# Gated blocks of a feed-forward net turned by VectorE squares and small DMAs in place of TensorE transposes

## The chip, the cores and the metric

One Trainium2 chip, one of its cores. The metric is the device time of one execution in microseconds. The kernel before takes 972.12 us, the median of three runs (972.08 to 974.28). The profile shown is of one further execution, which took 969.86 us.

## The reference, cut to what matters

The kernel computes a two-layer decoder trunk for 256 tokens of width 1024 in float32: a state-space layer and an attention layer, each between two half-weighted SwiGLU feed-forward nets (inner width 2816). The change touches only the four feed-forward nets:

```
def swiglu(x, w_in, w_out):
    g, u = jnp.split(x @ w_in, 2, axis=-1)
    return (jax.nn.silu(g) * u) @ w_out
...
h = h + 0.5 * swiglu(rmsnorm(h, ffn1_norm[layer]), ffn1_w_in[layer], ffn1_w_out[layer])
```

## The kernel before, in words

The work is a list of 13 phases, each a product of the 256 tokens with one streamed weight matrix. Four phases are called "in" (n = 0, 3, 7, 11: x @ w_in, 11 blocks of 512 columns, 8 tiles of the inner dimension) and each is followed by an "out" phase (n = 1, 4, 8, 12: @ w_out, 2 blocks, 22 tiles). Weights come in units of 128 x 1024 floats (two tiles of one block). An "in" block has 4 units, an "out" block 11.

Each float32 product is made of three products of fp32r parts. For each unit SyncE loads 512 KB into one of six `raw` buffers (L412), ScalarE writes the high part `w_hi` (`split`, L652), VectorE the rest `w_lo` (`split`, L931), and TensorE runs 12 matmuls for it (2 token halves x 2 tiles x 3 products, L1252). There are four slots for `w_hi` and `w_lo`. In each unit's step, ScalarE and VectorE split the unit that is three further on (`LEAD = 3`), and ScalarE waits first until TensorE has used the unit that had the slot before.

The order on each engine is written out by hand, as a loop over phase, block and unit. In the step of unit 0 of a block, ScalarE takes silu of the gate half of the block before from PSUM, once for each half of the tokens (`gate`, L672), and VectorE multiplies it with the other half and the inverse RMS into `prod` (`gated`, L970). `prod` has tokens on the partitions. The "out" phase needs it with the inner columns on the partitions, as `hid_hi` and `hid_lo`. Before the change TensorE does this: after unit 1 of blocks 4 and 8, and after unit 1 of the "out" phase, it transposes the last four (at the end three) blocks in a batch (`turn_hidden`, L1257: eight 64 x 128 transposes a block). ScalarE copies the PSUM result to `hid_hi` in fp32r (`high_hidden`, L680) and VectorE writes the difference to `hid_lo` (`low_hidden`, L982), spread over the steps after.

ScalarE's queue is in order: what is issued in one step stands ahead of all later splits. The state-space part lies between phases 1 and 2, and its tables are made by GpSimd, ScalarE and VectorE during phases 0 and 1.

Of the kernel before, what the change touches and what calls it, by code (L numbers as in the profile page):

```python
# [11 lines left out]
ALU = mybir.AluOpType  # L12
ACT = mybir.ActivationFunctionType
# [3 lines left out]

P = 128
HP = P // 2
TOK = 256  # L20
TT = TOK // P
D = 1024
# [42 lines left out]

X_OF = {2: [(2, 1)], 4: [(3, 0), (4, 1)], 8: [(5, 0)], 10: [(6, 0)]}
FINAL = 12
BATCH = 4
BATCHES = (0, 4, 8)
TABLE_AT = (1, 3, 5, 7, 9, 11, 12, 13, 14, 15, 16, 17)  # L70


# [35 lines left out]
    return [(phases[p.n - 1], phases[p.n - 1].blocks - 1, j)] if chained else []  # L108


def batch_behind(p, phases, b):

    if p.name == "in" and b in BATCHES[1:]:
        return p, range(b - BATCH, b)
    if p.name == "out" and b == 0:
        f = phases[p.n - 1]
        return f, range(BATCHES[-1], f.blocks)
    return p, range(0)


def high_behind(p, phases, b, j):

    if p.name == "in" and b in BATCHES[1:] and j >= 2:
        first = b - BATCH + 2 * (j - 2)
        return [(p, first), (p, first + 1)]
    if p.name == "out" and b == 0 and j in (2, 3):
        f = phases[p.n - 1]
        first = BATCHES[-1] + 2 * (j - 2)
        return [(f, c) for c in range(first, min(first + 2, f.blocks))]
    return []  # L130


def low_behind(p, phases, b, j):

    if p.name == "in" and b in BATCHES[1:] and j == 3:
        return [(p, b - BATCH)]
    if p.name == "in" and b - 1 in BATCHES[1:] and j >= 1:
        return [(p, b - 1 - BATCH + j)]
    if p.name == "out" and b == 0 and 3 <= j < 3 + phases[p.n - 1].blocks - BATCHES[-1]:
        return [(phases[p.n - 1], BATCHES[-1] + j - 3)]  # L140
    return []


def trunk(nc, io, out):
# [9 lines left out]
    def sem(name):  # L154
        return ctx.enter_context(nc.semaphore(name))

    with ctx:
# [99 lines left out]
        def w_columns(d):  # L257
            return w2[:, :, :, PPT * d:PPT * d + PPT, :].rearrange("p r s g j -> p (r s) g j")

        def prod_of(b):  # L260
            i = b % BATCH
            return prod[:, i] if i < 2 else prod2[:, i - 2]

        def halves(a):
            return a.rearrange("p (b h x) -> p b h x", h=2, x=HP)

        def turned_block(b):
            at, col = KT + b % BATCH // 2 * 2, b % 2 * HB
            return ps[:, at:at + 2, col:col + HB].rearrange("p h (b x) -> p b h x", x=HP)

        def z_place(d):
            i = d % Z_SLOTS
# [17 lines left out]
        def bank(gb, tok):  # L290
            return 2 * ((gb + 1) % 2) + tok
# [9 lines left out]
        drained = sem("drained")  # L301
        kq_drained = sem("kq_drained")
        act_ready = sem("act_ready")
        hid_turned = sem("hid_turned")
        hid_hi_done = sem("hid_hi_done")
        hid_ready = sem("hid_ready")

# [330 lines left out]
        def _(act):  # L638
# [7 lines left out]
            def split(gu):  # L646
                if gu >= len(units):
                    return
                act.wait_ge(landed[gu % RAW], 16 * (gu // RAW + (1 if gu % RAW else 0)))
                if gu >= WS:  # L650
                    act.wait_ge(unit_used, gu - WS + 1)
                act.activation(w_hi[:, gu % WS, :], raw[:, gu % RAW, :], ACT.Copy)\  # L652
                   .then_inc(hi_done, 1)
# [8 lines left out]
            def gate(p, b):  # L662
                for q in range(TT):
# [10 lines left out]
                    else:  # L674
                        act.activation(act_out[:, q, :], ps[:, bank(p.block0 + b, q), HB:NB],
                                       ACT.Sigmoid).then_inc(act_ready, 1)

            def high_hidden(p, b):
                act.wait_ge(hid_turned, p.hid0 + min(b // BATCH * BATCH + BATCH, p.blocks))
                act.activation(halves(hid_hi[:, 2 * b:2 * b + 2, :].rearrange("p f x -> p (f x)")),  # L680
                               turned_block(b), ACT.Copy).then_inc(hid_hi_done, 1)

            def squares(p, b, w):
                for q in range(TT):
# [44 lines left out]
            def dense(n, chained=True):  # L729
                p = phases[n]  # L730
                for b in range(p.blocks):
                    for j in range(p.upb):
                        for done in follow_ups(p, phases, b, j, chained):
                            after(*done)
                        for turned_one in high_behind(p, phases, b, j):
                            high_hidden(*turned_one)
                        if j < p.upb - (LEAD if n == 1 and b else 0) and (n, b, j) not in SPLIT_IN_S5:
                            split(p.unit0 + b * p.upb + j + LEAD)
                        if n == 0 and b == 0 and j == 3:
                            input_squares()  # L740
                        if n == 0 and b == 1 and j == 1:
                            s5_angles()
                        if n == 1 and b == 1 and 3 <= j < 3 + len(early_masks):
                            early_masks[j - 3]()
# [174 lines left out]
        def _(dve):  # L919
# [41 lines left out]
            def gated(p, b):  # L961
                for q in range(TT):
                    dve.wait_ge(act_ready, p.acts0 + TT * b + q + 1)
                    gb = p.block0 + b
                    if p.name == "in":
                        if b >= BATCH:
                            dve.wait_ge(hid_turned, p.hid0 + b - BATCH + 1)
                        elif p.hid0:
                            dve.wait_ge(hid_turned, p.hid0)
                        dve.scalar_tensor_tensor(prod_of(b)[:, q, :], ps[:, bank(gb, q), HB:NB],  # L970
                                                 rs[:, q:q + 1], act_out[:, q, :],
                                                 ALU.mult, ALU.mult).then_inc(drained, 1)
                    else:
                        cols = slice(HB * b, HB * b + HB)
                        link(dve.tensor_tensor(prod[:, 0, q, :], ps[:, bank(gb, q), 0:HB],
                                               act_out[:, q, :], ALU.mult))
                        dve.tensor_tensor(h[:, q, cols], h[:, q, cols], prod[:, 0, q, :], ALU.add)\
                           .then_inc(drained, 1)

            def low_hidden(p, b):  # L980
                dve.wait_ge(hid_hi_done, p.hid0 + min(b // 2 * 2 + 2, p.blocks))
                dve.tensor_tensor(halves(hid_lo[:, 2 * b:2 * b + 2, :].rearrange("p f x -> p (f x)")),  # L982
                                  turned_block(b),
                                  halves(hid_hi[:, 2 * b:2 * b + 2, :].rearrange("p f x -> p (f x)")
                                         .bitcast(F32)), ALU.subtract).then_inc(hid_ready, 1)

            def residual(p, b):
                for q in range(TT):
# [261 lines left out]
        def _(pe):  # L1250
# [3 lines left out]
            def turn(at, col, src):  # L1254
                for r in range(2):
                    rows = slice(HP * r, HP * r + HP)
                    last = pe.transpose(ps[:, at + r, col:col + HP], src[rows, :], ident[rows, rows])  # L1257
                return last

            def turn_hidden(f, batch):  # L1260
                if not batch:
                    return
                pe.wait_ge(drained, f.drained0 + TT * (batch[-1] + 1))
                if f.hid0 + batch[0]:
                    pe.wait_ge(hid_ready, f.hid0 + batch[0])
                if f.n == 7 and batch[0] == 0:
                    pe.wait_ge(kq_ready, 4)
                for b in batch:
                    for i in range(2):
                        for q in range(TT):  # L1270
                            last = turn(KT + b % BATCH // 2 * 2, b % 2 * HB + (2 * i + q) * HP,
                                        prod_of(b)[:, q, i * P:i * P + P])
                    last.then_inc(hid_turned, 1)

            def turn_h(p, c):

                t = turned[p.n, c]
# [70 lines left out]
            def dense(n, chained=True):  # L1348
                p = phases[n]
                for b in range(p.blocks):  # L1350
                    late = p.upb - left(p, b)
                    if (n, b) == (2, 0):
                        continue
                    for j in range(2 if (n, b) == (10, 0) else 0, p.upb):
                        if j == late:
                            for q in range(TT):
                                for i in range(late, p.upb):
                                    unit(p, b, i, (q,))
                        if j >= late:
                            continue  # L1360
                        unit(p, b, j)
                        for done in follow_ups(p, phases, b, j, chained):
                            after(*done)
                        if j == 1:
                            turn_hidden(*batch_behind(p, phases, b))
                        if n == 9 and b == 1 and j >= 2:
                            scores(j - 2)

# [249 lines left out]
```

## Time and profile before

| | |
|---|---|
| Median of three runs | 972.12 us |
| The profiled execution, its own time | 969.86 us |
| Its span in the trace | 967.7 us |
| TensorE busy (matmul) | 955.9 us, 99% |
| VectorE busy | 597.8 us, 62% |
| ScalarE busy | 499.8 us, 52% |
| GpSimd busy | 189.5 us, 20% |
| Queue of SyncE's loads | 167.79 MB, 54.5% of the 16 DMA engines' time |

The span is what the trace covers; 2.2 us of the execution's time lie around it. TensorE is busy almost throughout, so its matmuls are the line against which the others' delays count. An engine's share is a mean over stages: ScalarE and VectorE have idle time in each unit, and an instruction that makes DMAs counts as no busy time of its engine.

### The profile page before, as it was taken

The page shows a single profiled execution, that of the slowest core. Times are in us where ns is not written, and L with a number is a line of the kernel's source. Part 1 is how long each engine was busy: PE and PEld are TensorE (multiplying, and loading weights), DVE is VectorE, ACT ScalarE, POOL GpSimd, SP SyncE. Part 2 cuts the span into 40 slices and gives each one's busy share as a digit, 9 for nine tenths or more (in the row PEclk, how much of TensorE's full clock was granted, in tenths as well). Part 3 has the DMA queues.
Part 4 walks back from the last instruction along what each step waited for, and adds up shares of the span by engine and source line. Part 5 has one row for each costly group of instructions (what it writes and reads, how often), then busy time and mean ns, then how long its engine had stood idle before and what let it go on. Part 6 is the DMA issues. An engine that isn't in the chain of part 4 may idle for free.

```text
span 967.7 us, 15102 instructions
## 1 busy us (share of the span) xinstructions
PE 955.9 (99%) x6110; PEld 790.2 (82%) x6110; DVE 597.8 (62%) x744; ACT 499.8 (52%) x711; POOL 189.5 (20%) x235
## 2 busy tenths in 40 slices
PE   9999999999999999999999999999999999999997
PEld 7888888788788888888888888888888888888886
DVE  5565779889765554656555555555557555656544
ACT  7554544576555454545544454554458454545441
POOL 4899999800000000000000000000060000000000
PEclk9999999999999999999999999999999999999999
DMA  9766555520455655565566666656651366555551
GB/s 347 269 184 197 181 174 174 175 69 5 142 187 193 194 178 194 184 208 183 166 198 196 193 177 196 191 177 195 188 182 45 111 198 193 186 187 192 179 169 43
DMA packets 47557, 169.35 MB, mean 175 GB/s; under 512 B 5505, under 2 KB 5505, under 8 KB 47489
## 3 DMA queue, kind: packets, MB, share of 16 engines
q1 hardware_dynamic: 47056, 167.79, 54.5%
q8 instruction: 48, 0.79, 0.3%
q10 hardware_dynamic: 432, 0.61, 0.2%
q14 instruction: 21, 0.16, 0.1%
HBM read 167.33 MB, written 1.05 MB: 174 GB/s over the span
## 4 chain that ended last, share of the span: by engine, by line
PE 88%; DVE 8%; issue 2%; ACT 1%; DMA 1%; SPq 0%; POOLq 0%; POOL 0%; DVEq 0%; ACTq 0%
PE ps L1252 85%; DVE w_lo L931 2%; PE ps L1257 2%; DVE scan L1158 1%; DVE tmp L1087 1%; PE ps L1284 1%; DMA raw<-in_in 1%; DVE rot_b L1165 1%; DVE rot_a L1145 1%; DVE rot_b L1147 1%; ACT w_hi L652 0%; DVE rot_in L1154 0%; DVE states L1172 0%; PE ps L1297 0%; ACT pr L881 0%
## 5 line engine op out<-in xcount | busy, mean ns | idle before, releaser
L931 DVE TENSOR_TENSOR w_lo<-raw,w_hi 128x1024 fp32r<-128x1024 f32 x311 | 399.7, 1289 | 307.0 <-ACT w_hi L652 305.7
L652 ACT ACTIVATE w_hi<-raw 128x1024 fp32r<-128x1024 f32 x311 | 328.4, 1059 | 305.9 <-PE ps L1252 303.2
L1252 PE MATMUL ps<-w_hi,x_hi 128*128 128x512 f32 x896 | 352.4, 393 | 0.9 <-DVE w_lo L931 0.6
L1252 PE MATMUL ps<-w_hi,x_lo 128*128 128x512 f32 x896 | 349.3, 390 | 0.0
L1252 PE MATMUL ps<-w_lo,x_hi 128*128 128x512 f32 x896 | 349.2, 390 | 0.0
L1252 PEld LDWEIGHTS ps<-w_hi,x_hi 128*128 128x128 f32 x896 | 168.4, 188 | 37.2 <-DVE w_lo L931 1.4
L1252 PEld LDWEIGHTS ps<-w_hi,x_lo 128*128 128x128 f32 x896 | 168.3, 188 | 35.2
L1252 PEld LDWEIGHTS ps<-w_lo,x_hi 128*128 128x128 f32 x896 | 168.5, 188 | 34.0
L1252 PE MATMUL ps<-w_hi,hid_hi 128*128 128x512 f32 x352 | 138.1, 392 | 1.0 <-DVE w_lo L931 1.0
L1252 PE MATMUL ps<-w_lo,hid_hi 128*128 128x512 f32 x352 | 137.2, 390 | 0.0
L1252 PE MATMUL ps<-w_hi,hid_lo 128*128 128x512 f32 x352 | 137.2, 390 | 0.0
L466 POOL TENSOR_TENSOR ms<-ss 128x2 f32<-128x2 f32 x5 | 1.0, 203 | 528.6 <-ACT act_out L689 525.0
L1252 PEld LDWEIGHTS ps<-w_hi,hid_hi 128*128 128x128 f32 x352 | 66.1, 188 | 16.0 <-DVE w_lo L931 2.3
L1252 PEld LDWEIGHTS ps<-w_hi,hid_lo 128*128 128x128 f32 x352 | 66.1, 188 | 13.9
L1252 PEld LDWEIGHTS ps<-w_lo,hid_hi 128*128 128x128 f32 x352 | 66.1, 188 | 13.4
L672 ACT ACTIVATE act_out<-ps,rs 128x256 f32<-128x256 f32 x88 | 41.5, 475 | 45.5 <-PE ps L1252 45.4
L970 DVE SCALAR_TENSOR_TENSOR prod<-ps,rs,act_out 128x256 f32<-128x256 f32 x88 | 41.8, 480 | 19.7 <-ACT act_out L672 19.7
L680 ACT ACTIVATE hid_hi<-ps 128x512 fp32r<-128x512 f32 x44 | 24.1, 599 | 32.0 <-PE ps L1257 32.0
L634 POOL TENSOR_TENSOR rs<-end_ms,mhalf 128x1 f32<-128x1 f32 x2 | 1.1, 560 | 182.3 <-DVE end_ms L1241 182.3
L466 POOL TENSOR_TENSOR sm<-sm 128x32 f32<-128x32 f32 x64 | 34.3, 536 | 11.0 <-ACT sm L793 3.8
L982 DVE TENSOR_TENSOR hid_lo<-ps,hid_hi 128x512 fp32r<-128x512 f32 x44 | 30.0, 682 | 0.0
L466 POOL TENSOR_TENSOR tmp<-cp,sm 128x512 f32<-128x512 f32 x16 | 26.2, 1637 | 1.3
(151 smaller groups left out, 599.6 us busy)
## 6 DMA issues: line engine op xcount, KB each, us to landing
raw<-in_in SPq DMA_DIRECT2D x175, 512.0 KB, 4.3
raw<-in_out SPq DMA_DIRECT2D x88, 512.0 KB, 3.4
raw<-in_glu SPq DMA_DIRECT2D x16, 512.0 KB, 4.3
raw<-in_k SPq DMA_DIRECT2D x8, 512.0 KB, 4.4
raw<-in_v SPq DMA_DIRECT2D x8, 512.0 KB, 4.1
raw<-in_q SPq DMA_DIRECT2D x8, 512.0 KB, 4.4
raw<-in_o SPq DMA_DIRECT2D x8, 512.0 KB, 4.0
xt<-in_xt SPq DMA_DIRECT2D x4, 256.0 KB, 5.6
```

The lines of the kernel that those rows point to most:

```text
L466: link(pool.tensor_tensor(o, a, b, op))
L652: act.activation(w_hi[:, gu % WS, :], raw[:, gu % RAW, :], ACT.Copy)\
L672: act.activation(act_out[:, q, :], ps[:, bank(p.block0 + b, q), 0:HB], ACT.Silu, scale=rs[:, q:q + 1]).then_inc(act_ready, 1)
L680: act.activation(halves(hid_hi[:, 2 * b:2 * b + 2, :].rearrange("p f x -> p (f x)")), turned_block(b), ACT.Copy).then_inc(hid_hi_done, 1)
L931: dve.tensor_tensor(w_lo[:, gu % WS, :], raw[:, gu % RAW, :], w_hi[:, gu % WS, :].bitcast(F32), ALU.subtract)\
L970: dve.scalar_tensor_tensor(prod_of(b)[:, q, :], ps[:, bank(gb, q), HB:NB], rs[:, q:q + 1], act_out[:, q, :], ALU.mult, ALU.mult).then_inc( ...
L982: dve.tensor_tensor(halves(hid_lo[:, 2 * b:2 * b + 2, :].rearrange("p f x -> p (f x)")), turned_block(b), halves(hid_hi[:, 2 * b:2 * b + 2 ...
L1087: link(dve.tensor_tensor(part[k], t[:, groups, low], turn[i], ALU.mult))
L1145: dve.tensor_tensor(rot_a[:, :, :, :], v, table(rotc, d), ALU.mult)\
L1147: dve.tensor_tensor(rot_b[:, :, :, :], v, table(rots, d), ALU.mult)\
L1252: return pe.matmul(o, w, x, start=start, stop=stop, skip_group_check=True)
L1257: last = pe.transpose(ps[:, at + r, col:col + HP], src[rows, :], ident[rows, rows])
```

## The change

TensorE's transposes of the gated blocks (`turn_hidden`) are gone. A gated block of 256 x 256 is now turned in two steps. VectorE transposes the block's 32 x 32 squares in place, with one instruction of 128 x 512 elements at the end of `gated`; for this it first waits for its own two products of the block. Then ScalarE issues sixteen DMAs from SBUF to SBUF (`move_hidden`), one for each pair of 32-partition groups; each has 32 partitions x 4 runs x 32 floats (16 KB in runs of 128 bytes). They put the squares at their places in `hid_lo`. ScalarE issues them one unit after the step in which the block was gated, that is after the split in the step of unit 1 (in the first "in" phase the first block's are two units later). Four semaphores, one for each slot of the four blocks in flight, count the landings.

`high_hidden` now waits for a block's sixteen DMAs and reads `hid_lo` in SBUF; `low_hidden` subtracts in place in `hid_lo`. Both now come for one block at a time, in units 1 and 2 of the block two further on; the last two blocks of a phase in units 1 and 2 and units 4 and 5 of the "out" phase. `gated` waits for the DMAs of the block four before.

```diff
+def gate_unit(p, b):
+    return (b + 1) * p.upb + (2 if p.n == 0 and b == 0 else 0)
+
+def high_behind(p, phases, b, j):
+    if p.name == "in" and b >= 2 and j == 1:
+        return [(p, b - 2)]
+    if p.name == "out" and b == 0 and j in (1, 4):
+        return [(f, f.blocks - 2 + j // 4)]
...
+        def pieces(g, q, c):
+            return prod_of(g)[Q * q:Q * q + Q].rearrange("p t (a c x) -> p c (t a) x", a=2, x=Q)[:, c]
+        def places(b, q, c):
+            return hid_lo[Q * c:Q * c + Q, 2 * b:2 * b + 2, :].bitcast(F32)\
+                .rearrange("p i (t q x) -> p q (i t) x", t=TT, x=Q)[:, q]
...
+            def move_hidden(p, b):
+                g = p.hid0 + b
+                act.wait_ge(hid_squares, g + 1)
+                for q in range(QS):
+                    for c in range(QS):
+                        act.dma_start(places(b, q, c), pieces(g, q, c)).then_inc(hid_moved[g % SLOTS], 16)
+            moves = {p.unit0 + gate_unit(p, b) + MOVE_BEHIND: (p, b)
+                     for p in phases if p.name == "in" for b in range(p.blocks)}
             def high_hidden(p, b):
-                act.wait_ge(hid_turned, p.hid0 + min(b // BATCH * BATCH + BATCH, p.blocks))
-                act.activation(halves(hid_hi[...]), turned_block(b), ACT.Copy).then_inc(hid_hi_done, 1)
+                act.wait_ge(hid_moved[g % SLOTS], 16 * QS * QS * (g // SLOTS + 1))
+                act.activation(hid_hi[:, 2 * b:2 * b + 2, :], hid_lo[:, 2 * b:2 * b + 2, :].bitcast(F32),
+                               ACT.Copy).then_inc(hid_hi_done, 1)
...
                         if j < p.upb - (LEAD if n == 1 and b else 0) and (n, b, j) not in SPLIT_IN_S5:
                             split(p.unit0 + b * p.upb + j + LEAD)
+                        if p.unit0 + b * p.upb + j in moves:
+                            move_hidden(*moves[p.unit0 + b * p.upb + j])
...
+                if p.name == "in":
+                    dve.wait_ge(drained, p.drained0 + TT * (b + 1))
+                    whole = prod_of(p.hid0 + b).rearrange("p t x -> p (t x)")
+                    dve.transpose(whole, whole).then_inc(hid_squares, 1)
...
-                        if j == 1:
-                            turn_hidden(*batch_behind(p, phases, b))
```

## Rows read from the trace of the kernel before

**Rows 1.** The page: busy time, share of the span and instructions of each engine.

```profile
PE 955.9 (99%) x6110; PEld 790.2 (82%) x6110; DVE 597.8 (62%) x744; ACT 499.8 (52%) x711; POOL 189.5 (20%) x235
```

**Rows 2.** The chain in order of time: start us, us, what.

```profile
136.56 0.92 PE ps L1257 x16
...
338.78 1.15 PE ps L1257 x32
339.93 43.74 PE ps L1252 x192
...
417.70 0.90 PE ps L1257 x24
```

**Rows 3.** Most of phase 3: us, busy of PE, PEld, DVE, ACT, POOL, clock, DMA share, GB/s.

```profile
292.50:418.00 125.50, 125.50 (x617) 103.44 (x615) 70.51 (x77) 62.73 (x78) 1.08 (x4) 1.00 0.60 193
```

**Rows 4.** Waits in that stretch: us in total, times, longest us.

```profile
ACT w_hi L652 <- PE ps L1252: 44.1, 29, 1.7
```

**Rows 5.** Timeline of ScalarE: start us, us, line, operation.

```profile
333.38 0.47 ACT L672 ACTIVATE act_out<-ps,rs 128x256 f32<-128x256 f32 x1 [0.88 <-PE ps L1252]
333.75 1.05 ACT L652 ACTIVATE w_hi<-raw 128x1024 fp32r<-128x1024 f32 x1
336.16 1.06 ACT L652 ACTIVATE w_hi<-raw 128x1024 fp32r<-128x1024 f32 x1 [1.35 <-PE ps L1252]
...
340.94 1.06 ACT L652 ACTIVATE w_hi<-raw 128x1024 fp32r<-128x1024 f32 x1
341.89 1.08 ACT L680 ACTIVATE hid_hi<-ps 128x512 fp32r<-128x512 f32 x2
```

**Rows 6.** Timeline of VectorE in the same phase.

```profile
331.81 1.23 DVE L931 TENSOR_TENSOR w_lo<-raw,w_hi 128x1024 fp32r<-128x1024 f32 x1 [1.49 <-ACT w_hi L652]
332.95 0.48 DVE L970 SCALAR_TENSOR_TENSOR prod<-ps,rs,act_out 128x256 f32<-128x256 f32 x1
333.89 0.48 DVE L970 SCALAR_TENSOR_TENSOR prod<-ps,rs,act_out 128x256 f32<-128x256 f32 x1 [0.46 <-ACT act_out L672]
...
342.03 1.23 DVE L931 TENSOR_TENSOR w_lo<-raw,w_hi 128x1024 fp32r<-128x1024 f32 x1 [3.56 <-ACT w_hi L652]
```

**Rows 7.** SyncE's loads (min/median/max ns), then ScalarE's queue of DMAs beside its work.

```profile
L412 SPq DMA_DIRECT2D raw<-in_out x88: 327/328/328, 109.5 to 936.8; - x88
...
409.64 1.06 ACT L652 ACTIVATE w_hi<-raw 128x1024 fp32r<-128x1024 f32 x1 [1.66 <-PE ps L1252]
409.66 0.34 ACTq L871 DMA_DIRECT2D last_gain<-in_last_gain  x1
```

**Rows 8.** Timeline of SyncE's issues at the start, one behind the other.

```profile
2.17 0.43 SPq L416 DMA_DIRECT2D xt<-in_xt  x1
...
3.59 0.54 SPq L412 DMA_DIRECT2D raw<-in_in  x1
...
4.69 1.80 SPq L412 DMA_DIRECT2D raw<-in_in  x3
...
15.33 0.65 SPq L426 DMA_DIRECT2D w<-in_b  x1
16.02 0.60 SPq L426 DMA_DIRECT2D w<-in_c  x1
```

**Rows 9.** DMA queues from 2 to 4 us, then from 340 to 383 us.

```profile
q10 hardware_dynamic: 163, 0.04, 9.5%
...
q1 hardware_dynamic: 2192, 8.00, 57.8%
```

**Rows 10.** Issues of the whole run: KB each, median us to landing.

```profile
raw<-in_in SPq DMA_DIRECT2D x175, 512.0 KB, 4.3
...
out_x<-fin SPq DMA_DIRECT2D x4, 256.0 KB, 2.2
```

**Rows 11.** Groups by shape that stand for the new work.

```profile
L982 DVE TENSOR_TENSOR hid_lo<-ps,hid_hi 128x512 fp32r<-128x512 f32 x44 | 30.0, 682 | 0.0
L1158 DVE TENSOR_TENSOR_SCAN scan<-decay_even,rot_in 128x512 f32<-128x512 f32 x4 | 4.9, 1225 | 0.1
```

More of the change, by code:

```diff
@@ L19 @@
 HP = P // 2
+Q = 32
+QS = P // Q
 TOK = 256
@@ L67 @@
 FINAL = 12
-BATCH = 4
-BATCHES = (0, 4, 8)
+SLOTS = 4
+MOVE_BEHIND = 1
 TABLE_AT = (1, 3, 5, 7, 9, 11, 12, 13, 14, 15, 16, 17)
@@ L108, in follow_ups @@
     return [(phases[p.n - 1], phases[p.n - 1].blocks - 1, j)] if chained else []
[L111 to L115, printed above, removed]
-        f = phases[p.n - 1]
[L117 to L129, printed above, removed]
+def gate_unit(p, b):
[4 more added lines that the diff above has]
+    if p.name == "out" and b == 0 and j in (1, 4):
+        f = phases[p.n - 1]
+        return [(f, f.blocks - 2 + j // 4)]
     return []
 def low_behind(p, phases, b, j):
[L135 to L140, printed above, removed]
+    if p.name == "in" and b >= 2 and j == 2:
+        return [(p, b - 2)]
+    if p.name == "out" and b == 0 and j in (2, 5):
+        f = phases[p.n - 1]
+        return [(f, f.blocks - 2 + j // 5)]
     return []
@@ L258, in w_columns, with prod_of, tile_of @@
             return w2[:, :, :, PPT * d:PPT * d + PPT, :].rearrange("p r s g j -> p (r s) g j")
[L260 to L261 removed]
+        def prod_of(g):
+            i = g % SLOTS
             return prod[:, i] if i < 2 else prod2[:, i - 2]
+        def tile_of(g, q):
+            return prod_of(g).rearrange("p i (t x) -> p t i x", x=P)[:, q]
+        def pieces(g, q, c):
[3 more added lines that the diff above has]
+                .rearrange("p i (t q x) -> p q (i t) x", t=TT, x=Q)[:, q]
         def halves(a):
             return a.rearrange("p (b h x) -> p b h x", h=2, x=HP)
[L267 to L269 removed]
         def z_place(d):
@@ L303, in trunk @@
         act_ready = sem("act_ready")
-        hid_turned = sem("hid_turned")
+        hid_squares = sem("hid_squares")
+        hid_moved = [sem(f"hid_moved{i}") for i in range(SLOTS)]
         hid_hi_done = sem("hid_hi_done")
@@ L676, in gate @@
                                        ACT.Sigmoid).then_inc(act_ready, 1)
+            def move_hidden(p, b):
[6 more added lines that the diff above has]
+                     for p in phases if p.name == "in" for b in range(p.blocks)}
             def high_hidden(p, b):
-                act.wait_ge(hid_turned, p.hid0 + min(b // BATCH * BATCH + BATCH, p.blocks))
-                act.activation(halves(hid_hi[:, 2 * b:2 * b + 2, :].rearrange("p f x -> p (f x)")),
-                               turned_block(b), ACT.Copy).then_inc(hid_hi_done, 1)
+                g = p.hid0 + b
+                act.wait_ge(hid_moved[g % SLOTS], 16 * QS * QS * (g // SLOTS + 1))
+                act.activation(hid_hi[:, 2 * b:2 * b + 2, :], hid_lo[:, 2 * b:2 * b + 2, :].bitcast(F32),
+                               ACT.Copy).then_inc(hid_hi_done, 1)
             def squares(p, b, w):
@@ L965, in gated @@
                     if p.name == "in":
[L966 to L971, printed above, removed]
+                        g = p.hid0 + b
+                        if g >= SLOTS:
+                            dve.wait_ge(hid_moved[g % SLOTS], 16 * QS * QS * (g // SLOTS))
+                        dve.scalar_tensor_tensor(tile_of(g, q), halved(ps[:, bank(gb, q), HB:NB]),
+                                                 rs[:, q:q + 1], halved(act_out[:, q, :]),
                                                  ALU.mult, ALU.mult).then_inc(drained, 1)
@@ L978, in gated @@
                            .then_inc(drained, 1)
+                if p.name == "in":
+                    dve.wait_ge(drained, p.drained0 + TT * (b + 1))
+                    whole = prod_of(p.hid0 + b).rearrange("p t x -> p (t x)")
+                    dve.transpose(whole, whole).then_inc(hid_squares, 1)
             def low_hidden(p, b):
[L981 to L985, printed above, removed]
+                dve.wait_ge(hid_hi_done, p.hid0 + b + 1)
+                part = hid_lo[:, 2 * b:2 * b + 2, :]
+                dve.tensor_tensor(part, part.bitcast(F32), hid_hi[:, 2 * b:2 * b + 2, :].bitcast(F32),
+                                  ALU.subtract).then_inc(hid_ready, 1)
             def residual(p, b):
@@ L1258, in turn @@
                 return last
[L1260 to L1273, printed above, removed]
             def turn_h(p, c):
```

## The prediction

> **What bounds the kernel now.** I read the page's busy times first: TensorE is busy in 955.9 of 967.7 us [rows 1]. The chain of waits in order of time comes next, because it says whether that busy time is also the path. It is: through the "in" phases the chain is nothing but matmuls, and a batch of four blocks (16 units) takes 43.74 us, so 10.93 us a block and 2.73 us a unit [rows 2]. Between the batches stand the transposes of L1257, 1.15 us for four blocks. Then the table by stretch: in most of phase 3 TensorE is busy for all 125.5 us, VectorE for 70.5 and ScalarE for 62.7 [rows 3]. ScalarE's idle time is time in which it waits for TensorE to free a slot (44.1 us there) [rows 4], so ScalarE is off the path, with some 5.5 us idle per block of 10.93. Last, the timelines of ScalarE and VectorE show how far they run ahead, and the rows of DMA issues what sixteen of them cost.
>
> **What goes.** 352 transposes. In the chain they are eight batches of four blocks at 1.15 us and four batches of three at 0.90 to 0.92 us [rows 2]: 9.2 + 3.6 = 12.8 us, all on the path. That is the whole gain. ScalarE and VectorE lose waits for these transposes, which cost nothing before.
>
> **VectorE.** A block gets one transpose of 128 x 512. The trace has none. The nearest row is an elementwise instruction of the same 128 x 512, 0.68 us, the scan over as many elements takes 1.23 us [rows 11], and an instruction of half the elements 0.48 us [rows 6]: between 0.48 and 1.23 I take 0.69. `low_hidden` stays one instruction of 128 x 512. VectorE's sum per block rises from some 6.1 us (70.5 / 125.5 of 10.93) to 6.8, far below 10.93, so by its sum it costs nothing; by its place it matters (below). `high_hidden` from SBUF is of the same size as from PSUM; no price.
>
> The Trainium skill, "VectorE: DVE Perf Modes", section "The three transpose paths", gives 311 ns for 128 x 128 in bf16 as 32 x 32 squares; four times that would be an estimate of 1.24 us, the scan's price, and would add 0.55 us to each period below, some 22 us to the sum. No run so far shows it.
>
> **ScalarE.** A block gets sixteen DMA issues. A lone issue takes 0.33 us on SyncE's queue and 0.34 us on ScalarE's, and the latter began 0.02 us after the split ahead of it had begun: an issue lies beside ScalarE's instruction ahead of it, but nothing shows one beside an instruction behind it [rows 7]. Issues one behind the other are dearer: three steps from 2.17 to 3.59 us are 0.47 us each; with the DMA engines full three take 1.80 (0.60 each), and the two 3-dimensional ones step by 0.69 [rows 8]. So between 0.37 (a lone one and a gap of 0.04) and 0.69. I take 0.50, near the 0.47: 16 issues are 8.0 us, in which ScalarE has nothing new to do. Its idle time per block, 5.5 us, and the instructions queued ahead of the burst, one copy and one split (1.66 us), together cover 7.2. SyncE's four loads a block stay on their own queue.
>
> **The burst against the lead.** ScalarE's split in the step of unit 1 starts when TensorE ends unit 0 [rows 4, 5]; call this 0. The burst starts at 0.1. The next split's result is wanted when TensorE is four units on, at 10.93. After the burst come 1.06 us (split high), 0.03, 1.23 (split low) [rows 5, 6] and 0.05 of gap: 2.37. With 0.1 + 8.0 + 2.37 = 10.47 the first burst just fits, with 0.46 us to spare.
>
> The next one doesn't start on time. It waits for `hid_squares`, and what makes that ready is now itself behind the burst: two splits high, at 0.95 from start to start [rows 5]; their lows, so that the second low starts 2.2 us after the burst; 1.14 to the first product, some 0.38 to the second and its 0.48 [rows 6] (the silus fit beside); 0.69 for the transpose and 0.1 of gaps. Sum 2.2 + 1.14 + 0.38 + 0.48 + 0.69 + 0.1 = 5.0 us. So one loop of ScalarE and VectorE is 5.0 + 8.0 = 13.0 us against the 10.93 in which TensorE could do a block. Who waits: TensorE, for `w_lo` of unit 1, 13.0 - 10.93 = 2.07 us per block.
>
> Per phase ten bursts follow the first: 10 x 2.07 - 0.46 = 20.2 us; four phases 81. In phase 0 the first burst is two units late and the second comes two units behind it: 0.1 + 8.0 + 2.2 (silus and products, no splits between) + 8.0 + 2.37 = 20.7 against the 16.4 us of six units, 4.3 us late where the regular pattern is 1.6 late: 2.7 more. The last bursts stand in the "out" phase; `hid_hi` and `hid_lo` of block 10 are wanted only at its unit 10, 27 us on. Sum: +81 + 2.7 - 12.8 = +70.9 us. The traced execution took 969.86 us, so 1040.8; I say 1041 (the median of three lies 2.3 us above that execution, a run's scatter).
>
> **The DMA engines.** A block needs 128 runs of 128 bytes and 16 counts on each engine. Packets of at most 384 bytes took 9.5% of 16 engines over 2 us for 163, so 19 ns each [rows 9]: 144 x 0.019 = 2.7 us per engine and block at most, beside 57.8% of 10.93 = 6.3 us for the weights [rows 9]. The sum, 9.0, is below 10.93. From above the price is a packet of 4 KB, 0.578 x 43 x 16 / 2192 = 0.18 us, which would make 26 us. A burst's last landing is wanted four units after its start at the earliest, some 3 us after its end, and issues land after 2.2 to 4.3 us [rows 10]; `high_hidden` stands behind a late silu and a split by then, so this wait adds nothing at my price.
>
> The skill's "DMA: Bandwidth & Descriptors", "Rules for kernel authors", speaks against this change: under 64 KB a transfer is mostly overhead and should be coalesced, and each here has 16 KB. The rows agree as to the issue: 0.33 us for 512 KB, 0.34 for another, so the bytes don't make the price.
>
> **Rivals.** *The issues fit (faster).* If a burst's issues step at 0.37, the burst is 5.9 us, the loop 10.9, and TensorE never waits: 969.9 - 12.8 + 1 (phase 0) = 958. For it speaks that all loads in steady state take 0.33; against it that these have idle time ahead of them, and that every run of issues in the trace steps at 0.47 or more. It decides at 0.40: loop 11.4, 4 x (10 x 0.47 - 2.1) = 10.5 us of stalls and some 1 to 2 in phase 0, which is what the transposes gave. One more way to it: the sequencer could queue the next splits before the burst's issues and the engine run them meanwhile. "Advanced Engine Details and Errata", section "Sequencer and Instruction Queues" of the skill, says that other engine instructions can be queued while the sequencer's own code executes. Then the burst costs nothing. Rows 7 show a DMA beside the instruction ahead of it alone; I count both in this case's chance.
> *The issues are congested (slower still).* At 0.60 to 0.69, for the DMA engines carry loads throughout: at 0.60 the loop is 14.6, 4 x (10 x 3.67 + 1.1) = 151, with phase 0's 4 and less 12.8, +142: 1112.
> *The DMA engines bound it.* If runs of 128 bytes cost half a 4 KB packet, 0.09 us, they need 13 us, with the weights 19.3 per block: 4 x 10 x 8.4 - 13 = +322, 1290. Against it stand the 19 ns.
>
> **How the numbers follow.** Forecast 0.55 (its own range 990 to 1085: issues at 0.43 to 0.56), congested 0.19, DMA engines 0.04, issues fit 0.17, and 0.05 for a burst so near 0.40 that stalls and gain cancel. The range 955 to 1115 takes in the fit and leaves out the dearest issues and the DMA case. What a measurement can tell from no change is 0.3%, 3 us: faster 0.17, same 0.05, slower 0.78.
>
> **What would show it.** Right: in "in" phases TensorE waits for `w_lo` (L931) once a block, about 2 us, in unit 1; VectorE's wait there is on ScalarE's split; sixteen issues of ScalarE's queue step at 0.5 us with no ACTIVATE between; ScalarE no longer waits for TensorE in the step behind a burst; a block takes 13.0 us, the "out" phases keep their time. Wrong: ACTIVATEs of later splits beside the burst, a step of 0.37 or of 0.6, TensorE's block at 10.93, or `high_hidden` as the one that waits, for a DMA.

## The result and the profile after

The changed kernel takes 1177.45 us (median of four runs, 1175.45 to 1179.24); the kernel before took 973.2 us beside it. The ratio is 1.2097, with a 95% interval of 1.2066 to 1.2128. That is slower, as forecast, but by 204 us where 71 were forecast, and beyond the range's end of 1115.

First the page: busy times, the slices, the queues of the DMAs, and the chain by line.

```profile
span 1173.4 us, 15135 instructions
PE 1013.1 (86%) x5758; PEld 819.7 (70%) x5758; DVE 605.3 (52%) x788; ACT 482.8 (41%) x711; POOL 162.6 (14%) x235
PE   9688778999999788879999877877999997778887
q1 hardware_dynamic: 47056, 167.79, 45.8%
q10 hardware_dynamic: 101808, 12.19, 6.7%
PE ps L1270 39%; ACTq L686 35%; ACT w_hi L655 7%; ACT act_out L675 2%; DVE w_lo L947 2%; ACT hid_hi L694 1%; PE ps L1287 1%; DMA raw<-in_in 1%; PE ps L1403 0%; DVE prod L985 0%; DVE prod L997 0%; PE ps L1275 0%; PE ps L1300 0%; ACT pr L897 0%; ACTq L673 0%
```

TensorE fell from 99% [rows 1] to 86% busy, and its low slices are mostly those of the "in" phases. The chain has a new member with 35%: ScalarE's queue at L686, the line that issues the sixteen DMAs. ScalarE itself is less busy than before (41%), because an issue counts as no busy time: the busy table alone would call it idle. The DMA engines spend 6.7% of their time on the new queue (q10). So its 101,808 packets are cheap: (0.067 x 16 x 1173.4) / 101808 = 0.012 us, 12 ns each.

The loop of one block shows in ScalarE's timeline in phase 3 (start us, us, what):

```profile
426.45 1.05 ACT L655 ACTIVATE w_hi<-raw 128x1024 fp32r<-128x1024 f32 x1
427.37 10.65 ACTq L686 DMA_DIRECT2D hid_lo<-prod  x16
438.13 2.00 ACT L655 ACTIVATE w_hi<-raw 128x1024 fp32r<-128x1024 f32 x2 [10.64 <-issue]
440.04 0.82 ACT L675 ACTIVATE act_out<-ps,rs 128x256 f32<-128x256 f32 x2
440.75 1.05 ACT L655 ACTIVATE w_hi<-raw 128x1024 fp32r<-128x1024 f32 x1
441.70 0.62 ACT L694 ACTIVATE hid_hi<-hid_lo 128x512 fp32r<-128x512 f32 x1
442.22 1.05 ACT L655 ACTIVATE w_hi<-raw 128x1024 fp32r<-128x1024 f32 x1
443.14 7.16 ACTq L686 DMA_DIRECT2D hid_lo<-prod  x11
```

and in VectorE's for the same stretch:

```profile
439.22 2.36 DVE L947 TENSOR_TENSOR w_lo<-raw,w_hi 128x1024 fp32r<-128x1024 f32 x2 [9.03 <-ACT w_hi L655]
441.50 0.87 DVE L985 SCALAR_TENSOR_TENSOR prod<-ps,rs,act_out 128x256 f32<-128x256 f32 x2
442.40 0.71 DVE L997 STREAM_TRANSPOSE prod<-prod 128x512 f32<-128x512 f32 x1
```

No ACTIVATE stands beside the burst except the split ahead of it. The burst takes 10.65 us. Behind it come two splits, two products and the transpose, and the next burst starts 0.03 us after the transpose ends, at 443.14. One block therefore takes 443.14 - 427.37 = 15.77 us, of which 5.12 lie between the bursts, where 5.0 were worked out ahead. The issues step at 10.65 / 16 = 0.67 us. TensorE waits where it was said to, once a block, in unit 1 (the first unit whose split stands behind the burst), for the low part of the weights. The waits of TensorE over the run (us, count, longest):

```profile
PE ps L1270 <- DVE w_lo L947: 149.4, 45, 5.5
```

the issues of L686 (ns of one, min/median/max) with the time to their landing:

```profile
L686 ACTq DMA_DIRECT2D hid_lo<-prod x704: 592/622/1793, 29.8 to 1115.9; - x176
DMA to landing us min/median/max: 1.8/2.8/5.5
```

and the table of windows for exactly one loop (span, then busy us of PE, PEld, DVE, ACT, POOL, then granted clock, DMA share, GB/s):

```profile
427.37:443.14 15.77, 13.76 (x49) 10.84 (x48) 6.70 (x9) 5.13 (x8) 0.00 (x0) 0.82 0.55 148
```

No issue took less than 0.59 us. TensorE's 45 waits take 3.3 us in the mean (2.0 in this loop) and not 15.77 - 10.93 = 4.84, because its granted clock is 0.82 in that loop: behind the wait its first matmuls start 0.43 us apart, at the lower of its two levels, and the later ones 0.23. By this reading the clock costs nothing more here, for the loop of ScalarE and VectorE sets the 15.77 us.

What the loop adds can be compared with a whole phase. In the chain, phase 3 starts at 292.5 us before and at 352.9 after; the first matmul on `hid_hi`, with which phase 4 starts, and the last stand in these rows, of before and then of after:

```profile
L1252 PE MATMUL ps<-w_hi,hid_hi x88: 388/389/500, 412.1 to 473.3; 128*128 128x512 f32 x88
```

```profile
L1270 PE MATMUL ps<-w_hi,hid_hi x88: 389/389/677, 511.7 to 581.0; 128*128 128x512 f32 x88
```

The "in" phase grew from 119.6 to 158.8 us, the "out" phase from 61.2 to 69.3 (the last two bursts stand there): +47.3 us. The loop's formula with the measured burst gives 10 x (15.77 - 10.93) + 2.2 - 3.2 = 47.4: ten loops, the 2.2 us by which the first burst is now late (0.1 + 10.65 + 2.37 - 10.93), and the transposes that are gone. From phase 3 to the end the span grew by 145 of its 206 us, 48.4 for each of three pairs of phases.

The other 60.4 us lie ahead of phase 3, where the same formula gives 50, with the 2.6 us that phase 0 has for its second burst (two units behind the first). The rest shows in VectorE's row behind a burst of phase 0, which ScalarE starts at 125.22 us, while GpSimd works:

```profile
136.99 3.92 DVE L947 TENSOR_TENSOR w_lo<-raw,w_hi 128x1024 fp32r<-128x1024 f32 x2 [6.21 <-ACT w_hi L655]
```

The two splits that took 2.36 us in phase 3 take 3.92 here. They lie in the loop, and the next burst starts at 142.47: a loop of 17.25 us.

### The profile page after: what moved, and what is told of

It is laid out like the page before. It is cut to its first block, busy times and chain, and to the rows that moved or that the text cites. A ratio compares the mean times of both kernels' runs of the same rounds, so it can differ in the third digit from the quotient of the medians.

```text
span 1173.4 us, 15135 instructions
## 1 busy us (share of the span) xinstructions
PE 1013.1 (86%) x5758; PEld 819.7 (70%) x5758; DVE 605.3 (52%) x788; ACT 482.8 (41%) x711; POOL 162.6 (14%) x235
## 3 DMA queue, kind: packets, MB, share of 16 engines
q10 hardware_dynamic: 101808, 12.19, 6.7%
## 4 chain that ended last, share of the span: by engine, by line
PE 41%; ACTq 35%; ACT 12%; issue 8%; DVE 3%; DMA 1%; POOL 0%; SPq 0%; POOLq 0%; DVEq 0%
PE ps L1270 39%; ACTq L686 35%; ACT w_hi L655 7%; ACT act_out L675 2%; DVE w_lo L947 2%; ACT hid_hi L694 1%; PE ps L1287 1%; DMA raw<-in_in 1%; PE ps L1403 0%; DVE prod L985 0%; DVE prod L997 0%; PE ps L1275 0%; PE ps L1300 0%; ACT pr L897 0%; ACTq L673 0%
## 5 line engine op out<-in xcount | busy, mean ns | idle before, releaser
L947 DVE TENSOR_TENSOR w_lo<-raw,w_hi 128x1024 fp32r<-128x1024 f32 x311 | 385.6, 1264 | 506.8 <-ACT w_hi L655 505.6
L1270 PE MATMUL ps<-w_hi,x_hi 128*128 128x512 f32 x896 | 377.1, 421 | 123.5 <-DVE w_lo L947 123.4
L1270 PE MATMUL ps<-w_lo,x_hi 128*128 128x512 f32 x896 | 368.7, 411 | 0.0
L1270 PE MATMUL ps<-w_hi,x_lo 128*128 128x512 f32 x896 | 367.3, 410 | 0.0
L1270 PEld LDWEIGHTS ps<-w_hi,x_hi 128*128 128x128 f32 x896 | 180.6, 202 | 178.2 <-DVE w_lo L947 139.4
L1270 PEld LDWEIGHTS ps<-w_hi,x_lo 128*128 128x128 f32 x896 | 180.4, 201 | 40.6
L1270 PEld LDWEIGHTS ps<-w_lo,x_hi 128*128 128x128 f32 x896 | 181.1, 202 | 37.6
L1002 DVE TENSOR_TENSOR hid_lo<-hid_lo,hid_hi 128x512 fp32r<-128x512 f32 x44 | 35.1, 798 | 0.0
L997 DVE STREAM_TRANSPOSE prod<-prod 128x512 f32<-128x512 f32 x44 | 31.3, 712 | 1.5
L694 ACT ACTIVATE hid_hi<-hid_lo 128x512 fp32r<-128x512 f32 x44 | 27.4, 622 | 0.0
```

The source lines that it names most:

```text
L694: act.activation(hid_hi[:, 2 * b:2 * b + 2, :], hid_lo[:, 2 * b:2 * b + 2, :].bitcast(F32), ACT.Copy).then_inc(hid_hi_done, 1)
L947: dve.tensor_tensor(w_lo[:, gu % WS, :], raw[:, gu % RAW, :], w_hi[:, gu % WS, :].bitcast(F32), ALU.subtract)\
L997: dve.transpose(whole, whole).then_inc(hid_squares, 1)
L1002: dve.tensor_tensor(part, part.bitcast(F32), hid_hi[:, 2 * b:2 * b + 2, :].bitcast(F32), ALU.subtract).then_inc(hid_ready, 1)
L1270: return pe.matmul(o, w, x, start=start, stop=stop, skip_group_check=True)
```

## The experiments

The first six share one frame. ScalarE's copy and VectorE's subtraction read `prod` instead of `hid_lo`, and `gated` waits for that copy instead of the DMAs, so that these can be changed at will; they leave out the assembly of the turned blocks. Their bursts stand where the change has them. The kernel before took 969.91 us beside the first four, 969.87 beside the other two. The kernels without DMAs, two and two, by pairs, and the hybrid were timed four times; each other changed kernel of this section once, so that 2 or 3 us between two of them tell nothing.

**No DMAs.**

```diff
             def move_hidden(p, b):
-                for q in range(QS):
-                    for c in range(QS):
-                        act.dma_start(places(b, q, c), pieces(g, q, c)).then_inc(hid_moved[g % SLOTS], 16)
+                return
             def high_hidden(p, b):
-                act.wait_ge(hid_moved[g % SLOTS], 16 * QS * QS * (g // SLOTS + 1))
+                act.wait_ge(hid_squares, g + 1)
```

> The changed kernel without its sixteen DMAs; VectorE's transpose of the squares stays. ScalarE and VectorE read the squares straight from prod, so the hidden values aren't at their right places: the assembly of the squares is left out. Theory (ScalarE's burst of issues delays the splits, and nothing else in the change costs): no burst, so only the 12.8 us of TensorE's transposes go: 957 to 961 us, a block of an in phase takes 10.93 us. Rival (the in-place transpose, its wait on VectorE's own products, or the reads from SBUF cost): above 972 us.

Measured: 965.07 us, ratio 0.9935 (0.9915 to 0.9955). The whole loss is gone with the DMAs, so VectorE's transpose and the reads from SBUF are not what made the kernel slow. But only about 5 of the 12.8 us came: a time between the two theories' numbers. I come back to that with the last experiment.

**Eight of the sixteen.** `for c in range(QS)` becomes `for c in range(2)`.

> As the run without DMAs, but with eight of the sixteen DMAs of each block, in a burst at the same place (half of the block isn't moved; ScalarE and VectorE read from prod). Theory (loop of a block = 5.1 us of splits, products and transpose + issues x 0.667 us): 5.1 + 8 x 0.667 = 10.4 us, below TensorE's 10.93, so no stall: 957 to 966 us. Rival (each DMA costs its share whatever the burst's length, by the DMA engines or by landing): half of the loss stays, near 1068 us.

Measured: 966.21 us. Eight issues cost 1 us over none, which is within the scatter; sixteen cost 202 to 203 in the same frame (the next two runs). This is a threshold and not a price per DMA.

**One run of 512 bytes instead of four of 128.**

```diff
-                        act.dma_start(places(b, q, c), pieces(g, q, c)).then_inc(hid_moved[g % SLOTS], 16)
+                        i, a = c // 2, c % 2 * P
+                        act.dma_start(hid_lo[Q * q:Q * q + Q, 2 * b + i, a:a + P].bitcast(F32),
+                                      prod_of(g)[Q * q:Q * q + Q, i, a:a + P])\
+                           .then_inc(hid_moved[g % SLOTS], 16)
```

> Sixteen DMAs per block in the same burst, of the same 16 KB and the same 32 partitions each, but each partition's 512 bytes in one run (two dimensions instead of three, 32 runs instead of 128; nothing is put at its turned place). Theory A (the pattern of an issue sets its price): issues step at 0.37 to 0.5 us, which gives 958 to 1040 us by the loop of 5.1 + 16 x step; at 0.47 it gives 1027. Theory B (issues of ScalarE's queue one behind the other cost 0.67 whatever they carry): 1165 to 1185 us.

**128 partitions x one run of 128 bytes.**

```diff
-                for q in range(QS):
-                    for c in range(QS):
-                        act.dma_start(places(b, q, c), pieces(g, q, c)).then_inc(hid_moved[g % SLOTS], 16)
+                for k in range(QS * QS):
+                    i, a = k // 8, k % 8 * Q
+                    act.dma_start(hid_lo[:, 2 * b + i, a:a + Q].bitcast(F32), prod_of(g)[:, i, a:a + Q])\
+                       .then_inc(hid_moved[g % SLOTS], 16)
```

> Sixteen DMAs per block in the same burst, two-dimensional, each 128 partitions x one run of 128 bytes: as many runs of the same length as in the changed kernel, but two dimensions instead of three. If the third dimension makes an issue dear: as with one run of 512 bytes, 958 to 1040 us and an issue of 0.33 to 0.45 us. If the number of runs makes it dear: issues of 0.6 us and 1165 to 1185 us.

Measured: 1168.26 and 1167.47 us. The issues, of the flat runs and then of the columns (min/median/max ns):

```profile
L688 ACTq DMA_DIRECT2D hid_lo<-prod x704: 513/612/2061, 29.2 to 1110.2; - x176
```

```profile
L687 ACTq DMA_DIRECT2D hid_lo<-prod x704: 472/622/1794, 29.2 to 1109.7; - x176
```

Medians of 0.61 and 0.62 us against 0.62: neither the third dimension nor the number of runs makes the price of an issue behind another, within these shapes. Theory A fell. The shape does show in the first issue of a burst, and there alone: 0.51 us for the flat runs, 0.47 for the columns, 0.59 in the changed kernel. What was left: being one behind the other, or reading SBUF.

**The same burst, read from HBM.**

```diff
-                        act.dma_start(hid_lo[Q * q:Q * q + Q, 2 * b + i, a:a + P].bitcast(F32),
-                                      prod_of(g)[Q * q:Q * q + Q, i, a:a + P])\
+                        act.dma_start(pad[Q * q:Q * q + Q, 24 * c:24 * c + 24],
+                                      io["in0"][b, Q * q:Q * q + Q, P * c:P * c + 24])\
```

> As the run with flat runs of 512 bytes (sixteen DMAs in one burst on ScalarE's queue, hidden values read from prod), but the DMAs bring 32 partitions x 96 bytes from HBM instead of moving 16 KB from SBUF; the squares aren't moved. Theory A (an issue that reads SBUF is dear, and one that reads HBM costs 0.33 us as a load does): steps of 0.37 to 0.47 us, the loop 11.0 to 12.6 us, 966 to 1030 us. Theory B (an issue with another directly ahead or behind costs 0.6 us, whatever it reads): steps of 0.6 to 0.66 us and 1120 to 1175 us.

Measured: 1056.37 us (before: 969.87). The burst's issues:

```profile
L687 ACTq DMA_DIRECT2D pad<-in_in x704: 317/443/1922, 29.1 to 998.6; - x176
```

and two bursts in ScalarE's timeline:

```profile
403.12 8.55 ACTq L687 DMA_DIRECT2D pad<-in_in  x16
...
416.79 7.63 ACTq L687 DMA_DIRECT2D pad<-in_in  x16
```

The answer lies between the theories. Of these issues that read HBM the first of a burst takes 0.32 us and the later ones 0.44; of the flat ones that read SBUF, 0.51 and 0.61. Bursts of 7.6 to 8.6 us are the 0.50 a step that I had forecast, and the time of 1056 us is near the forecast's 1041. So both hold: standing behind another costs 0.10 to 0.13 us in these two shapes, and these copies from SBUF cost nearly 0.2 more than those from HBM. This run also changes the number of bytes (96 a partition, not 512) and the tile written, so that the source alone makes the difference is likely and not shown. An issue of the original shape from HBM wasn't tried.

**Twelve in the burst.** `range(3)` in place of `range(2)` of the run with eight.

> As the run with eight DMAs in the burst, but with twelve. Theory (loop of 5.1 us + issues x 0.66 us): 13.0 us a block against TensorE's 10.93, so 10 x 2.1 - 0.5 = 20 us for each of four phases: 1045 to 1060 us. Rival (the loss grows in proportion from eight to sixteen): 1070 us. Rival (each issue costs alike from the first): 1120 us.

Measured: 1060.12 us, against 966.21 with eight and 1168 with sixteen (the two shapes above, in the same frame). The burst and what stands behind it:

```profile
429.77 7.87 ACTq L687 DMA_DIRECT2D hid_lo<-prod  x12
437.74 2.00 ACT L656 ACTIVATE w_hi<-raw 128x1024 fp32r<-128x1024 f32 x2 [7.84 <-issue]
```

That is the theory's upper end, 1060. The proportional rival's 1070 is near, and this one time doesn't tell the two apart; the rival of 1120 is out. What tells the threshold is the eight, at 966. The burst shown is one of the shorter ones: the eleven of phase 3 take 7.80 to 8.87 us, 8.18 in the mean. With that the loop is 13.30 us and the formula gives 4 x (10 x 2.37 - 0.3) = 94 over the 966 of no stall, so 1060. The chains agree: phase 3 starts at 324.9 us here and at 300.9 with eight, 24 us later, and each of the three later pairs of phases is 23 us longer.

**The same sixteen DMAs, four behind each of four splits.** From here on the kernels do the whole computation. The kernel before took 970.47 us beside this one, the next two (SyncE's queue, two and two) and the one by pairs; 969.87 beside the one with two places moved and the hybrid.

```diff
+def lane_of(k):
+    return 1 + k // 4, "act"
...
-                        if p.unit0 + b * p.upb + j in moves:
-                            move_hidden(*moves[p.unit0 + b * p.upb + j])
+                        for one in moves.get(p.unit0 + b * p.upb + j, ()):
+                            move(act, *one)
...
+    return hidden_at(p, phases, b, j, 6)
...
+    return hidden_at(p, phases, b, j, 7)
```

The last two lines put `high_hidden` six and `low_hidden` seven units behind the block's gate.

> The whole computation, with the same sixteen DMAs of each block still issued by ScalarE, but four behind the split of each of four steps instead of sixteen behind one; the copy to hid_hi comes one unit later. Theory (what costs is a burst that holds up the next splits and products, 10.7 us in one piece): four issues take 2.7 us, as long as TensorE's unit, so ScalarE just keeps up or falls behind by the silus' share: 966 to 1000 us. Rival (sixteen issues cost ScalarE 4.8 us a block wherever they stand): 1160 us or more.

Measured: 980.85 us. The same 704 issues on the same queue, at 0.61 us in the median, make the kernel 10 us slower than before instead of 204. Two steps of ScalarE:

```profile
423.71 1.06 ACT L677 ACTIVATE w_hi<-raw 128x1024 fp32r<-128x1024 f32 x1 [1.18 <-issue]
423.73 2.55 ACTq L418 DMA_DIRECT2D hid_lo<-prod  x4
...
430.08 1.06 ACT L677 ACTIVATE w_hi<-raw 128x1024 fp32r<-128x1024 f32 x1 [1.21 <-PE ps L1284]
430.10 2.55 ACTq L418 DMA_DIRECT2D hid_lo<-prod  x4
```

The issues begin 0.02 us after the split, beside it, so each split in front hides 1.06 us of them, and the rest fits about into TensorE's 2.73 us a unit. Not everywhere: where silus or a copy stand in the step too, ScalarE falls behind, and TensorE's waits (us, count, longest) keep a remainder:

```profile
PE ps L1284 <- DVE w_lo L961: 17.4, 24, 2.3
```

**The burst on SyncE's queue.** `lane_of` returns `1, "sp"`; SyncE issues a step's DMAs behind the load of nine units on.

> The whole computation, with each block's burst of sixteen DMAs issued by SyncE's queue between its loads instead of ScalarE's. Theory: SyncE now needs 16 x 0.65 + 4 x 0.33 to 0.6 = 11.7 to 12.8 us for a block of 10.93; loads come late and TensorE waits for a weight load by 0.8 to 1.9 us a block: 990 to 1045 us, and ScalarE keeps its idle time. Rival (the DMAs themselves, on the DMA engines, cost the time): 1150 us or more.

Measured: 1144.44 us, 100 us above the theory's range and near the rival's number, but not for its reason. SyncE's issues, and what ScalarE and VectorE do behind the burst:

```profile
401.77 10.27 SPq L420 DMA_DIRECT2D hid_lo<-prod  x16
412.08 4.39 SPq L437 DMA_DIRECT2D raw<-in_in  x4
416.52 10.27 SPq L420 DMA_DIRECT2D hid_lo<-prod  x16
```

```profile
413.28 0.63 ACT L710 ACTIVATE hid_hi<-hid_lo 128x512 fp32r<-128x512 f32 x1 [9.61 <-DMA hid_lo<-prod]
413.82 2.94 ACT L679 ACTIVATE w_hi<-raw 128x1024 fp32r<-128x1024 f32 x3
```

```profile
414.89 1.22 DVE L963 TENSOR_TENSOR w_lo<-raw,w_hi 128x1024 fp32r<-128x1024 f32 x1 [8.02 <-ACT w_hi L679]
```

The last of the four loads starts at 416.14, when VectorE's split has freed its buffer, and the next burst behind it. So there is a loop again, of 14.75 us, and it goes through the landing: burst, landing (1.2 us after its end), copy to `hid_hi`, ScalarE's split, VectorE's split, load, burst. The theory had counted the issues of SyncE and not what its queue waits for.

**Two and two.** `lane_of` returns `1 + k // 4, ("act", "sp")[k % 2]`.

> The whole computation; in each of four steps ScalarE issues two of a block's sixteen DMAs and SyncE two. Theory: 1.3 us a step on either queue, within TensorE's 2.73: no stall from issues, the time of the run without DMAs, 963 to 968 us. Rival (the DMA traffic or its landings cost something by themselves): clearly above the run without DMAs, 975 us or more.

Measured: 1033.76 us, ratio 1.0646 (1.0622 to 1.0669): far above the theory's 968, and by its number the rival's. ScalarE's waits in the two runs, SyncE alone and then both:

```profile
ACT hid_hi L710 <- DMA hid_lo<-prod: 431.2, 44, 12.1
```

```profile
ACT hid_hi L708 <- DMA hid_lo<-prod: 305.5, 44, 10.0
```

ScalarE waits for a landing once a block, 431 / 44 = 9.8 and 6.9 us. SyncE's share stood in order behind a load that waits for VectorE's split of three units on, this for ScalarE's, and ScalarE's stands behind the copy that waits for the landing. The next run moves only SyncE's share, two loads earlier.

```diff
-                for one in sp_moves.get(gu - LEAD - RAW, ()):
+                for one in sp_moves.get(gu - RAW - 1, ()):
```

> As the run in which ScalarE and SyncE issue two DMAs each in four steps, but SyncE's stand two loads earlier in its queue (behind the load of seven units on, not nine). Theory (that run was slow because SyncE's share waited behind loads that wait for VectorE, so that the copy to hid_hi waited for a landing): 963 to 972 us. Rival (two queues that issue at once, or SyncE's loads held up by its own share, cost the time): 1020 us or more.

Measured: 966.17 us, as without any DMAs (965.07). Two places in a queue were worth 68 us, and the same traffic on the same two queues costs nothing. ScalarE still waits for a landing once a block, but for 1.3 us (59.0 us in 44 times) and off the path: the DMA engines and the landings are cleared.

**One DMA for two blocks,** sixteen per pair, all by ScalarE, four behind each of four splits.

```diff
-            return prod_of(g)[Q * q:Q * q + Q].rearrange("p t (a c x) -> p c (t a) x", a=2, x=Q)[:, c]
+            src = (prod, prod2)[b // 2 % 2][Q * q:Q * q + Q, 0:b % 2 + 1]
+            return src.rearrange("p n i (t c x) -> p c (n i t) x", t=TT, x=Q)[:, c]
```

> The whole computation; one DMA carries the piece of two neighbouring blocks (32 partitions x 8 runs of 128 bytes), so sixteen per two blocks, issued by ScalarE alone, four behind the split of each of four steps. Theory A (an issue costs 0.65 us whatever it carries): half the issue time per block, 963 to 970 us. Theory B (an issue costs by its runs): steps of 1.3 us, so as much as sixteen issues a block, and no better than the run that spreads them.

Measured: 964.14 us, ratio 0.9932 (0.9914 to 0.995), with twice the runs in an issue:

```profile
L423 ACTq DMA_DIRECT2D hid_lo<-prod x384: 592/621/1552, 33.0 to 912.7; - x192
```

Theory A holds: 0.62 us for 256 runs as for 128. This kernel beats the kernel before, by about 6 us, but like the run without DMAs it has only about half of the 12.8. Where the rest went shows in VectorE's groups of that kernel, from 30 to 130 us (GpSimd makes the state-space tables) and from 400 to 500 us (GpSimd idle):

```profile
L966 DVE TENSOR_TENSOR w_lo<-raw,w_hi 128x1024 fp32r<-128x1024 f32 x35 | 54.5, 1572 | 21.5 <-ACT w_hi L682 21.4
L1021 DVE TENSOR_TENSOR hid_lo<-hid_lo,hid_hi 128x512 fp32r<-128x512 f32 x8 | 9.7, 1212 | 0.0
...
L966 DVE TENSOR_TENSOR w_lo<-raw,w_hi 128x1024 fp32r<-128x1024 f32 x37 | 44.8, 1221 | 36.0 <-ACT w_hi L682 36.0
L1021 DVE TENSOR_TENSOR hid_lo<-hid_lo,hid_hi 128x512 fp32r<-128x512 f32 x5 | 3.4, 677 | 0.0
```

and in the kernel before, from 30 to 130 us:

```profile
L982 DVE TENSOR_TENSOR hid_lo<-ps,hid_hi 128x512 fp32r<-128x512 f32 x8 | 5.4, 678 | 0.0
```

The same subtraction, reading SBUF for both inputs, takes 1.21 us beside a working GpSimd and 0.68 alone. Reading PSUM for one of them, it took 0.68 beside GpSimd too. GpSimd's tables are what VectorE and then TensorE need before the state-space part. So the last version leaves that phase as it was.

**A hybrid.** Phase 0 turned by TensorE as before, phases 3, 7 and 11 by pairs.

```diff
-        for b in range(1, p.blocks + 1, 2) if p.name == "in" else ():
+        for b in range(1, p.blocks + 1, 2) if p.name == "in" and p.n else ():
...
             def high_hidden(p, b):
+                if p.n == 0:
+                    act.wait_ge(hid_turned, min(b // BATCH * BATCH + BATCH, p.blocks))
+                    act.activation(halves(hid_hi[:, 2 * b:2 * b + 2, :].rearrange("p f x -> p (f x)")),
+                                   turned_block(b), ACT.Copy).then_inc(hid_hi_done, 1)
+                    return
...
                         if j == 1:
+                            turn_hidden(*batch_behind(p, phases, b))
```

> The whole computation: in the first in phase, beside which GpSimd makes the state-space tables, TensorE's transposes as in the kernel before; in the three others VectorE's squares and one DMA per two blocks as in the run with pairs. Theory (in the first phase the new way loses some 9 us, because VectorE's extra work from SBUF and GpSimd's slow each other; in the others it gains 3.2 us each): 9 to 10 us below the kernel before, 959 to 962 us. Rival (the 9 us have nothing to do with the first phase's way of turning): as the run with pairs, 964 us.

Measured: 960.25 us against 969.87, ratio 0.9892 (0.9873 to 0.9912). This is the fastest version of all. A line of its page:

```profile
PE 943.9 (99%) x5846; PEld 781.4 (82%) x5846; DVE 615.3 (64%) x777; ACT 497.4 (52%) x711; POOL 189.1 (20%) x235
```

and of TensorE's waits (us, count, longest):

```profile
PE ps L1339 <- DVE w_lo L1003: 1.3, 3, 0.7
```

TensorE waits for weights 1.3 us in all. The gain of 9.6 us is that of three phases at 3.2 us of transposes [rows 2]; its interval, 8.5 to 12.3 us, leaves room, and in the two profiled executions the stretch from phase 3 to the end is 11.7 us shorter, 3.9 for each pair of phases. Against the pairs everywhere the hybrid gains another 4 us: in phase 0 the new way costs more than the transposes did. Which share of phase 0's loss is the subtraction and which the transpose or GpSimd's own slower instructions wasn't taken apart.

## Why the prediction was right and wrong

- *TensorE's transposes are worth 12.8 us on the path*: right in size for the three later phases (9.6 in the hybrid). In phase 0 their removal gave nothing, even with the burst out of the way: by pairs that phase lost some 4 us against TensorE's transposes. The prediction didn't count that VectorE's new work there stands beside GpSimd's.
- *VectorE's transpose, 0.69 us*: 0.71 measured, near the 0.68 of an elementwise instruction of the same 128 x 512. The estimate of 1.24 us, four times the 311 ns that the Trainium skill's "VectorE: DVE Perf Modes" gives for 128 x 128 in bf16 ("The three transpose paths"), doesn't hold for this instruction.
- *`low_hidden` stays one instruction of 128 x 512*, at the price that it had: right for phases 3, 7 and 11 (0.68 us), wrong in phase 0 (1.21).
- *The loop: burst plus 5.0 us*: right outside phase 0, 5.12 measured. That each later burst delays TensorE by the loop's excess over 10.93 held at eight issues (no excess, no loss), at twelve and at sixteen. The first burst didn't just fit: at 10.65 us it is 2.2 us late.
- *A burst steps at 0.50 us*: this is the step that failed. It measured 0.67: the burst is 10.65 us and not 8.0, the stall 4.84 us a block and not 2.07. Put into the prediction's own sum, with the measured loop, 4 x (10 x (15.77 - 10.93) + 2.2) + 2.6 - 12.8 = 192 us, against the 204 measured. So the longer burst accounts for 117 of the 133 us by which the forecast was short, and the 0.12 us more between the bursts for 5. Of what is left, some 10 us lie ahead of phase 3, where VectorE's splits beside GpSimd lengthen the loop. The price was read from loads of HBM. The copies read SBUF, of which the trace of before had no row, and I took the 0.60 in [rows 8] for congestion, though the 0.60 and the 0.69 there should have been kept as bounds of the likeliest case. The range's end of 1115 stands for a step of about 0.60, so it left out the upper part of the prediction's own "between 0.37 and 0.69". Each 0.01 us in the step is 6.4 us of time, 40 loops of 16 issues; a term with such leverage deserved the widest range, not the likeliest value's. The rival "the issues are congested" had the right step; at 0.67 its own formula gives 1162 us. Its cause isn't borne out: with SyncE's loads beside them as well, the copies from HBM stepped at 0.48 to 0.53 us.
- *The DMA engines have room*: right. 12 ns a packet in place of the 19 taken, and 964 to 981 us with all of the traffic once it is issued in small groups. The Trainium skill's "DMA: Bandwidth & Descriptors" asks in "Rules for kernel authors" to coalesce transfers under 64 KB; the trace agrees as to the number of issues (0.62 us for 16 KB and for 32 KB), and shows that what costs here is the issuing queue's time.
- *The rival in which the sequencer queues the next splits before the burst*: out. The first ACTIVATE behind the burst shown starts 0.11 us after its last issue ends.

## What to carry to other kernels

In these traces nothing that stands behind an issue of ScalarE's in its order starts before the issue ends (0.11 us after the burst of 10.65 us), and ScalarE's busy time doesn't show it. Count issues times their price against the lead that its consumers have, and put them in small groups behind instructions that run long; the same sixteen cost 204 us in one piece and 10 in four. Fewer, larger transfers did better than both: an issue's price didn't grow with the runs in it. Before a transfer is put on another in-order queue, look what that queue's next instruction waits for, and whether the chain comes back to the transfer.

## What the runs showed that was not expected

- An issue of a copy that reads SBUF takes 0.61 to 0.62 us behind another on ScalarE's queue, in all four shapes, and 0.60 on SyncE's. The first of a burst takes 0.47 to 0.59, by its shape. A copy from HBM takes 0.32 first and 0.44 behind another.
- The 128-byte packets from SBUF to SBUF cost the DMA engines about 12 ns each (6.7% of 16 engines over 1173.4 us for 101,808).
- The step in time from eight to sixteen issues is not linear: 966, 1060, 1168 us at 8, 12, 16.
- VectorE's subtraction of two SBUF operands is 1.8 times as long beside a busy GpSimd (1212 against 677 ns), its split 1.29 times (1572 against 1221). The split was longer beside GpSimd in the kernel before too (1441 against 1224), its subtraction from PSUM was not.
